# Routing one-hots of four tokens by one VectorE comparison, weights applied by ScalarE, three slots for U's rounded blocks

## What is computed

```python
sv, si = lax.top_k(s, PEER_TOPK)                       # per half, 16 of 128 keys
cand = sv[:, :, 0, :, None] + sv[:, :, 1, None, :]     # 16 x 16 sums
fv, fpos = lax.top_k(cand, PEER_TOPK)
g = jax.nn.softmax(fv, axis=-1)                        # (token, 128 picks)
a = gelu(einsum('ted,td->te', u_tab[eidx], hb))
y = einsum('te,ted->td', g * a, v_tab[eidx])
```

## Time and profile before

| | |
|---|---|
| median of 3 runs | 3866.59 us (3866.22 to 3867.75) |
| profiled execution, its own time | 3845.11 us |
| its span | 3843.3 us, mean granted TensorE clock 0.946 |
| TensorE matmuls busy | 3599.3 us (94%), 17636 records |
| VectorE busy | 2037.1 us (53%) |
| ScalarE busy | 1313.2 us (34%) |
| GpSimd busy | 790.2 us (21%) |

### The profile page before, as it was taken

One profiled execution on the slowest core, in us unless ns is written; L12 is line 12 of the kernel. 1 busy time (PEld: TensorE's weight loads), 2 busy tenths in 40 slices (PEclk: granted clock), 3 DMA queues, 4 the chain that ended last, 5 costly groups with the idle time before them and its releaser, 6 DMA issues.

```text
span 3843.3 us, 44509 instructions
## 1 busy us (share of the span) xinstructions
PE 3599.3 (94%) x17636; PEld 2988.7 (78%) x17636; DVE 2037.1 (53%) x4109; ACT 1313.2 (34%) x2117; POOL 790.2 (21%) x492
## 2 busy tenths in 40 slices
PE   6778988988999898999899999999999999999999
PEld 5456888877888777888766787888888888888887
DVE  5785545454332534332676466867757035555555
ACT  3343333333322424222444324343525232222222
POOL 0000010000000110000020023435353554444443
PEclk8888889889999979999988999999999999999999
DMA  3012111122332312332210234444444465656654
GB/s 103 29 51 66 50 50 50 52 97 83 98 99 93 104 55 84 97 99 88 78 57 1 83 108 146 164 149 158 152 157 173 143 212 188 191 188 208 193 187 139
DMA packets 192210, 434.96 MB, mean 113 GB/s; under 512 B 18114, under 2 KB 59330, under 8 KB 189955
## 3 DMA queue, kind: packets, MB, share of 16 engines
q1 hardware_dynamic: 181762, 398.54, 32.6%
q0 software_dynamic: 10240, 33.56, 2.3%
HBM read 362.84 MB, written 69.21 MB: 112 GB/s over the span
## 4 chain that ended last, share of the span: by engine, by line
PE 86%; DVE 9%; ACT 2%; issue 1%; POOL 1%; DMA 0%; DVEq 0%; SPq 0%; ACTq 0%
PE bank L321 19%; PE bank L2356 18%; PE bank L2063 17%; PE bank L324 13%; PE bank L2154 4%; PE bank L898 2%; PE bank L908 2%; PE bank L850 1%; PE bank L1687 1%; PE bank L862 1%; DVE acc L1090 1%; POOL etl L2052 1%; PE bank L432 1%; PE bank L1628 1%; DVE mix L729 1%
## 5 line engine op out<-in xcount | busy, mean ns | idle before, releaser
L280 DVE TENSOR_TENSOR wl<-raw,wh 128x1024 fp32r<-128x1024 f32 (+3 forms) x239 | 293.9, 1233 | 687.6 <-ACT wh L265 687.5
L265 ACT CAST wh<-raw 128x1024 fp32r<-128x1024 f32 (+3 forms) x239 | 246.9, 1036 | 673.0 <-PE bank L321 356.9
L2399 DVE TENSOR_TENSOR coefl<-gl,coefh 128x512 fp32r<-128x512 f32 x128 | 312.4, 2441 | 262.3 <-ACT coefh L2379 262.1
L2063 PE MATMUL bank<-peerhh,eth 128*128 128x512 f32 x1024 | 402.5, 393 | 9.4 <-POOL etl L2052 9.4
L2052 POOL TENSOR_TENSOR etl<-eu,eth 128x1024 fp32r<-128x1024 f32 x128 | 320.3, 2502 | 442.2 <-ACT eth L2048 442.0
L2063 PE MATMUL bank<-peerhh,etl 128*128 128x512 f32 x1024 | 398.9, 390 | 0.0
L2063 PE MATMUL bank<-peerhl,eth 128*128 128x512 f32 x1024 | 398.5, 389 | 0.0
L2356 PE MATMUL bank<-vsh,coefh 128*128 128x512 f32 x1024 | 398.3, 389 | 0.0
L2356 PE MATMUL bank<-vsl,coefh 128*128 128x512 f32 x1024 | 398.3, 389 | 0.0
L2356 PE MATMUL bank<-vsh,coefl 128*128 128x512 f32 x1024 | 398.3, 389 | 0.0
L2415 POOL TENSOR_TENSOR vsl<-vb,vsh 128x1024 fp32r<-128x1024 f32 x128 | 307.7, 2404 | 376.5 <-ACT vsh L2377 376.5
(11 more groups left out here) (551 smaller groups left out, 7481.9 us busy)
## 6 DMA issues: line engine op xcount, KB each, us to landing
eu<-in_peer_u SPq DMA_DIRECT2D x128, 512.0 KB, 3.7
vb<-in_peer_v SPq DMA_DIRECT2D x128, 512.0 KB, 4.0
acts<-eg POOLq DMA_DIRECT2D x128, 256.0 KB, 2.3
coefs<-stage SPq DMA_DIRECT2D x16, 2048.0 KB, 7.3
gd<-coefs SPq DMA_DIRECT2D x16, 2048.0 KB, 10.8
gl<-acts SPq DMA_DIRECT2D x128, 256.0 KB, 4.2
raw<-in_ada_w SPq DMA_DIRECT2D x48, 512.0 KB, 3.9
raw<-in_ffn_w_gate SPq DMA_DIRECT2D x44, 512.0 KB, 3.7
```

What stands on the lines that cost most here:

```text
L265: act.copy(parts_of(c)[0], raw_of(c)).then_inc(*up("w rounded", c))
L280: dve.tensor_tensor(lo, raw_of(c), hi.bitcast(F32), ALU.subtract).then_inc(*up("w split", c))
L2063: t = pe.matmul(b, tb[un][:, k * 128:(k + 1) * 128], peer_h[hn][:, k, :], start=k == 0 and i == 0, stop=k == 7 and i == 2)
L2399: dve.tensor_tensor(Cb[j % 4][1], gl[j % 5], Cb[j % 4][0].bitcast(F32), ALU.subtract).then_inc(*up("coef split", j))
```

## The change

- **VectorE** makes the one-hots of four tokens with one `tensor_tensor` comparison of 128 x 512 for each half, of a spread key list and four spread columns of `trs`. The weight is no longer part of it. 256 `tensor_tensor` take the place of 1024 `tensor_scalar`. The event is called "places".
- **ScalarE** multiplies the second half of each token by its weight, in place: four `activation(Copy, scale=pointer)` of 128 x 128 for each group m of four tokens (`weigh`), 512 in all. In its order stand: `weigh(0)` of the tile after the Exp, then for each m `weigh(m + 1)`, the wait for group m's matmuls ("pairs full"), the copy of L2192, and after every fourth group the unit.
- **TensorE** does the same matmuls, with one wait and one increment for a group.
- The one-hots lie in three slots of 4 KB + 4 KB (12 tokens) in place of 15 slots of one token.
- **U**: three pairs Et in place of two; ScalarE rounds and GpSimd subtracts block j + 2 in place of j + 1 before they turn to unit j. Two load buffers Eu in place of three, and two Gelu buffers Eg in place of four. SyncE's load of block j waits for the subtraction of block j - 2 in place of j - 3.

```diff
@@ -2014,15 +2014,16 @@
     iot, iob = gb0[:, 0:128], gb0[:, 0:16]
     trs = [gb0[:, 144 + i * 128:272 + i * 128] for i in range(3)]
     stage = [f("stage", 96 + 16 * i, 4096).rearrange("p (j t) -> p j t", j=128) for i in range(2)]
-    onehots = [f("oh", 128 + i, 256) for i in range(10)] + [gb0[:, 528:784]]
-    onehots += [place(f"onehot{i}", AT_SPLIT + 20 + i, [128, 256])[:, :] for i in range(4)]
+
+    onehots = [[x[:, 512 * h:512 * h + 512].rearrange("p (t n) -> p t n", t=4) for h in range(2)]
+               for x in (f("oh", 128, 1024), f("oh", 132, 1024), place("onehot2", AT_RAW + 36, [128, 1024])[:, :])]
...
-    Eu = [place(f"eu{q}", AT_RAW + 4 * q, [128, 1024])[:, :] for q in range(3)]
-    Et = [[place(f"et{n}{q}", AT_RAW + 12 + 8 * q + 4 * h, [128, 1024], R32)[:, :] for h, n in enumerate("hl")]
-          for q in range(2)]
-    Eg = [place(f"eg{q}", AT_RAW + 28 + 2 * q, [128, 512])[:, :] for q in range(4)]
+    Eu = [place(f"eu{q}", AT_RAW + 4 * q, [128, 1024])[:, :] for q in range(2)]
+    Et = [[place(f"et{n}{q}", AT_RAW + 8 + 8 * q + 4 * h, [128, 1024], R32)[:, :] for h, n in enumerate("hl")]
+          for q in range(3)]
+    Eg = [place(f"eg{q}", AT_RAW + 32 + 2 * q, [128, 512])[:, :] for q in range(2)]
     Vb = [f("vb", 32 + 4 * q, 1024) for q in range(3)]
     Vs = [[place(f"vs{n}{q}", AT_PHASE + 44 + 8 * q + 4 * h, [128, 1024], R32)[:, :] for h, n in enumerate("hl")]
           for q in range(4)]
@@ -2035,25 +2036,27 @@
 
 
     def sp_u(sp, on_sp, j):
-        if j < 3:
+        if j < 2:
             on_sp.wait_ge(*at("w split", max(c for c in range(N_PIECES) if c % 4 == j)))
         else:
-            on_sp.wait_ge(*at("u split", j - 3))
-        sp.dma_start(Eu[j % 3], I["peer_u_2"][j]).then_inc(*up(f"u in {j % 3}", j, by=16))
+            on_sp.wait_ge(*at("u split", j - 2))
+        sp.dma_start(Eu[j % 2], I["peer_u_2"][j]).then_inc(*up(f"u in {j % 2}", j, by=16))
 
     def act_u(act, on_act, j):
-        on_act.wait_ge(*at(f"u in {j % 3}", j))
-        if j >= 2:
-            on_act.wait_ge(*at("act full", j - 2))
-        act.copy(Et[j % 2][0], Eu[j % 3]).then_inc(*up("u rounded", j))
+        on_act.wait_ge(*at(f"u in {j % 2}", j))
+        if j >= 3:
+            on_act.wait_ge(*at("act full", j - 3))
+        else:
+            on_act.wait_ge(*at("w split", N_PIECES - 1))
+        act.copy(Et[j % 3][0], Eu[j % 2]).then_inc(*up("u rounded", j))
 
     def pool_u(pool, on_pool, j):
         on_pool.wait_ge(*at("u rounded", j))
-        pool.tensor_tensor(Et[j % 2][1], Eu[j % 3], Et[j % 2][0].bitcast(F32),
+        pool.tensor_tensor(Et[j % 3][1], Eu[j % 2], Et[j % 3][0].bitcast(F32),
                            ALU.subtract).then_inc(*up("u split", j))
 
     def pe_activate(pe, on_pe, j):
-        tb = Et[j % 2]
+        tb = Et[j % 3]
         b, before = banks.take(("act", j), ("gelu", j))
         for what in before:
             on_pe.wait_ge(*at(*what))
@@ -2066,13 +2069,13 @@
 
     def act_gelu(act, on_act, j):
         on_act.wait_ge(*at("act full", j))
-        if j >= 4:
-            on_act.wait_ge(*at(f"act out {j % 4}", j - 4))
-        act.activation(Eg[j % 4], banks["act", j], ACT.Gelu).then_inc(*up("gelu", j))
+        if j >= 2:
+            on_act.wait_ge(*at(f"act out {j % 2}", j - 2))
+        act.activation(Eg[j % 2], banks["act", j], ACT.Gelu).then_inc(*up("gelu", j))
 
     def pool_store(pool, on_pool, j):
         on_pool.wait_ge(*at("gelu", j))
-        pool.dma_start(Ad[j], Eg[j % 4]).then_inc(*up(f"act out {j % 4}", j, by=16))
+        pool.dma_start(Ad[j], Eg[j % 2]).then_inc(*up(f"act out {j % 2}", j, by=16))
 
     class Units:
 
@@ -2099,8 +2102,8 @@
 
     def act_units(act, on_act):
         def one(j):
-            if j + 1 < NJ:
-                act_u(act, on_act, j + 1)
+            if j + 2 < NJ:
+                act_u(act, on_act, j + 2)
             act_gelu(act, on_act, j)
         return Units(one)
 
@@ -2148,13 +2151,12 @@
                     b, before = banks.take(("g", tt, part, q), ("staged", tt, part, q))
                     for what in before:
                         on_pe.wait_ge(*at(*what))
+                    oi, oj = onehots[n % 3]
+                    on_pe.wait_ge(*at("onehot", n))
                     for x in range(4):
-                        oi, oj = onehots[n % 15][:, 0:128], onehots[n % 15][:, 128:256]
-                        on_pe.wait_ge(*at("onehot", n))
-                        pe.matmul(b[:, x * 128:(x + 1) * 128], oi, oj, start=True,
-                                  stop=True).then_inc(*up("onehot used", n))
-                        n += 1
-                    ev.same(("g full", tt, part, q), ("onehot used", n - 1))
+                        t = pe.matmul(b[:, x * 128:(x + 1) * 128], oi[:, x, :], oj[:, x, :], start=True, stop=True)
+                    t.then_inc(*up("pairs full", n))
+                    n += 1
                     if q % 16 == 12:
                         units()
 
@@ -2173,6 +2175,15 @@
             act.copy(kT[:, g * 4:g * 4 + 4, :], banks["pkT", g].rearrange("p (a b) -> p a b", a=4)).then_inc(
                 *up("copied act", "pkT", g))
         act_u(act, on_act, 0)
+        act_u(act, on_act, 1)
+
+        def weigh(m):
+            on_act.wait_ge(*at("places", m))
+            for x in range(4):
+                c = m % 32 * 4 + x
+                oj = onehots[m % 3][1][:, x, :]
+                t = act.activation(oj, oj, ACT.Copy, scale=trs[2][:, c:c + 1])
+            t.then_inc(*up("onehot", m))
         for tt in range(NT):
             for g in range(4):
                 on_act.wait_ge(*at("bank full", "scores", tt, g))
@@ -2183,9 +2194,13 @@
             units(16)
             on_act.wait_ge(*at("dve step", "route", tt, "less top"))
             act.activation(sw, sw, ACT.Exp).then_inc(*up("route exp", tt))
+            weigh(32 * tt)
             for part in range(4):
                 for q in range(0, 32, 4):
-                    on_act.wait_ge(*at("g full", tt, part, q))
+                    m = 32 * tt + 8 * part + q // 4
+                    if m % 32 != 31:
+                        weigh(m + 1)
+                    on_act.wait_ge(*at("pairs full", m))
                     n = 4 * tt + part
                     if n >= 2:
                         on_act.wait_ge(*at(f"coefs out {part % 2}", (n - 2) // 4, (n - 2) % 4))
@@ -2295,22 +2310,20 @@
             on_dve.wait_ge(*at("bank full", "ijg", tt))
             dve.tensor_copy(gb0[:, 144:528], banks["ijg", tt][:, 0:384]).then_inc(*up("ijg", tt))
             on_dve.wait_ge(*at("ijg", tt))
-            for part in range(4):
-                for q in range(0, 32, 4):
-                    for x in range(4):
-                        c = part * 32 + q + x
-                        oi, oj = onehots[n % 15][:, 0:128], onehots[n % 15][:, 128:256]
-                        if n >= 15:
-                            on_dve.wait_ge(*at("onehot used", n - 15))
-                        dve.tensor_scalar(oi, iot, trs[0][:, c:c + 1], 0.0, ALU.is_equal, ALU.add)
-                        dve.tensor_scalar(oj, iot, trs[1][:, c:c + 1], trs[2][:, c:c + 1], ALU.is_equal,
-                                          ALU.mult).then_inc(*up("onehot", n))
-                        n += 1
-    ROUTED = [("onehot used", 511), ("staged", 3, 3, 28), ("coefs out 0", 3, 2), ("coefs out 1", 3, 3)]
+            for m in range(32):
+                if n >= 3:
+                    on_dve.wait_ge(*at("pairs full", n - 3))
+                for half in range(2):
+                    t = dve.tensor_tensor(onehots[n % 3][half], iot.unsqueeze(1).to_broadcast([128, 4, 128]),
+                                          trs[half][:, 4 * m:4 * m + 4].unsqueeze(2).to_broadcast([128, 4, 128]),
+                                          ALU.is_equal)
+                t.then_inc(*up("places", n))
+                n += 1
+    ROUTED = [("pairs full", 127), ("staged", 3, 3, 28), ("coefs out 0", 3, 2), ("coefs out 1", 3, 3)]
     V_AHEAD = 4
 
     def sp_experts(sp, on_sp, units):
@@ -2324,7 +2337,7 @@
             if j >= 3:
                 on_sp.wait_ge(*at("v split", j - 3))
             sp.dma_start(Vb[j % 3], Vd[:, j, :]).then_inc(*up(f"v in {j % 3}", j, by=16))
-            on_sp.wait_ge(*at(f"act out {j % 4}", j))
+            on_sp.wait_ge(*at(f"act out {j % 2}", j))
             if j >= 5:
                 on_sp.wait_ge(*at("coef split", j - 5))
             sp.dma_start(gl[j % 5], Ad[j]).then_inc(*up(f"acts in {j % 5}", j, by=16))
@@ -2415,9 +2428,10 @@
             pool.tensor_tensor(Vs[j % 4][1], Vb[j % 3], Vs[j % 4][0].bitcast(F32),
                                ALU.subtract).then_inc(*up("v split", j))
         pool_u(pool, on_pool, 0)
+        pool_u(pool, on_pool, 1)
         for j in range(NJ):
-            if j + 1 < NJ:
-                pool_u(pool, on_pool, j + 1)
+            if j + 2 < NJ:
+                pool_u(pool, on_pool, j + 2)
```

## The result

The change makes the kernel slower. Four runs of it took 3941.88 to 3953.97 us, median 3943.7; with one more run beside them the kernel before has a median of 3866.4. The ratio is 1.0215 with a 95% interval of 1.0183 to 1.0247; a second comparison on another occasion gave 1.0237 (1.0201 to 1.0272). The medians differ by 77 us, and on that other occasion by 93. The forecast was 3965 us, 99 more than before, with a range of 3925 to 4035.

The account below looks back on a forecast made before the run. It took TensorE to bound placing, with VectorE level. 79 (rhythm) + 10 (starts) + 16 (clock) - 6 (U) = 99 us, added to the median 3866.6, gave about 3965 us, range 3925 to 4035.

Parts of the forecast that it names:

- The rhythm: Placing, unit to unit: 12.3 us in place of 9.46, ScalarE's weighings queued behind the Gelu; 79 us in all.
- One weighing: ScalarE multiplying one-hots by their weights: 0.27 us for one, 1.08 for four; ends 0.20 and 0.40.
- Rival 2: Small ScalarE instructions don't overlap in place: 0.40 us in place of 0.27, 44 us more, 4009; chance 0.07.
- The starts: Start of each placing stage: first unit 2.4 us later after the copy of L2296, four times, 10 us.
- The clock: TensorE in placing: idle stretches between groups may bring half clock; 16 us (0 to 70).
- Rival 1: Clock swings in the placing stages (L2063, L2154): full 70 us, 54 more than in the sum, 4019; chance 0.12.
- U's three slots: TensorE's waits for the subtraction of L2052, 9.4 us in six places, go except for the first block; -6 us.
- TensorE as the bound before: Placing rhythm of 9.46 us: TensorE never idle, 66.20 of 66.20 us, VectorE level; fewer waits costed at nothing.
- rival 3: Weighing hides under the products, TensorE stays the bound: 3870 us, or 3860 with free starts; chance 0.05.
- Rival 4: VectorE's comparison is no cheaper, spread operands running slower: 1.2 us more at each start, 3970; chance 0.03.

Follow-up runs that it names:

- the filling: The changed kernel plus three useless 128-column products in TensorE's idle gaps before the second to fourth group of each four: median 3934.42 us, ratio 1.0214 to the kernel before.

## Why the prediction was right, step by step

**The mechanism** held: ScalarE's place in the chain, with three weighings and two copies behind the Gelu, is shown by the chain after and by the run with another order. The total was 99 us forecast and 94.8 us in the traces, 77 and 93 in the two sets of timed runs. That the total came so close is in part luck: the terms below missed by +7 (rhythm), -8 (clock), +2 (starts) and -5 us (U), and the misses cancel.

- **The rhythm**, +2.8 forecast, +3.09 measured (12.54 to 9.45): 86 us in place of 79. The products of the last group with their handing over take 0.14 + 1.13, where I had 1.1. By the chain, with the Gelu at 0.5 as forecast, weighings and tail take 3.39 for 3.37, copies 1.87 for 1.8.
- **One weighing.** Four take 1.26 us (2434.97 above) and one alone 0.39, as line L2185 shows (ns, minimum/median/maximum):

```profile
...
L2185 ACT ACTIVATE oh<-oh,gb x344: 379/392/423, 2369.0 to 3070.1; 128x128 f32<-128x128 f32 x172
...
```

The period is (1.26 - 0.39) / 3 = 0.29, where I took 0.27. The estimate of 0.29 from the figures of the Trainium skill ("ScalarE: Activation LUTs", What ACT_TABLE_LOAD costs) was the better price. The sum hardly felt it, because a copy overlaps its neighbours more: from the start of one weighing, over the copy, to the start of the next ScalarE takes 2.00 us (2434.97 to 2436.97), where I had 1.98. Rival 2 (no overlap, 0.40) is refuted.
- **The starts**, +10 forecast. Against the kernel with U's part alone they are some 12 us longer (409.7 to 397.6). From the copy of the turned columns to the unit it is 2.4 to 3.2 us more in each tile, where I had 2.4.
- **The clock**, 16 forecast, 7 to 9 measured in the rhythms by the filling. Rival 1 was half right: the clock does swing, in 10 to 13 of 28 rhythms, but a swing costs at most 0.9 us. In the stretch shown it falls on one group and a short piece of the unit. The 2.5 us that I set as its most was too high even as a bound: it adds the loss on the unit (1.7) to the one on the products (about 1), though one low stretch of 3.4 us can't cost both in full. The Trainium skill's case of a clock that alternates because of short idling between groups of matmuls ("TensorE: Matmul & The Clock Gate", A second HAM failure mode: psum-queue depth-cycling) agrees with the granted clock here, 0.87 to 0.99 in the stretched rhythms and 1.00 in the others.
- **U's three slots**, -6 forecast, -11 measured. This term was mis-sized: I took the first block's wait off a sum of 9.4 us that did not hold it (the first of the six waits is at 2307 us, the first unit at 2261.86). Another 1.7 us went with them, and no view tells where they lay. The two load buffers cost TensorE nothing: ScalarE waits for a load of U in eight places, 11.5 us in all, but no wait of TensorE comes of it.
- **TensorE as the bound before** was a step that failed. I read 66.20 of 66.20 us busy as TensorE at its pace, and costed the fewer waits at nothing. It was VectorE that held 9.46, and its 65.64 us beside it should have been a warning; TensorE can do 9.03. It did not enter the sum, since the new rhythm is not bound by either. But the forecast so missed that cheaper comparisons were worth 28 x 0.42 = 12 us, if only the weights stay off ScalarE, and that rival 3 had a larger prize than it named.
- Rival 3's condition (at most 0.15 us for the weighing of four tokens) was not met: one such weighing took 1.06 us or more in the chain. Rival 4 falls with the comparison's 0.69 us; two take 1.30, a period of 0.6 as costed.

One correction to the description of the change: a slot of four tokens takes 2 KB of each partition for each half, 4 KB in all, not 4 KB + 4 KB.

## What to carry to other kernels

Work moved to an engine with idle time is free only if it stands in that engine's order at the place where it idles: ScalarE had 2.9 us to spare in front of each Gelu, and the weights that TensorE needed stood behind it. Before counting busy time, write down what is queued behind each long wait, and who needs it. And where two engines look level, measure the pace of each without the other: here the one that looked full had 0.4 us to spare in each rhythm.

## What was not expected of the hardware

- Records of short matmuls overlap (0.27 us each, starts 0.11 us apart), so a TensorE that waits 0.2 us for the next pair looks fully busy: 66.20 of 66.20 us in a stretch that VectorE held at 9.46 us a rhythm, when the same work can be done in 9.03.
- Useless matmuls in gaps of about 1 us raised the granted clock and took 8 to 10 us off the routing, with TensorE busy 921.22 us in place of 869.67.
- Back to back on 128 columns, ScalarE's copies with a pointer as scale follow every 0.29 us, and a copy of 512 columns behind them 1.17 us after the first of four; the next weighing starts 0.83 us after the start of such a copy, which takes 1.03 to 1.05.
